# Stacked rotary query parts, one stage for the latent norms and turns, and a reordered opening in a two-block transformer kernel

## The chip, the cores and the metric

The kernel runs on one core of one Trainium2 chip. The metric is the device time of one execution in microseconds (us). TensorE (PE) multiplies matrices and accumulates in PSUM banks; VectorE (DVE) and ScalarE (ACT) read PSUM and SBUF; SyncE (SP) issues nearly all DMAs; GpSimd (POOL) does little here.

## The reference, cut to what matters

Two transformer blocks follow one another on 512 latent and 256 context rows of width 1024. The changed code lies in the first block's opening (its modulation) and in the attention of the second block's last layer, multi-head latent attention:

```python
def mla_mixer(h_ctx, h_lat, ctx_queries, w_down, q_norm, kv_norm, w_uq, w_ukv, w_o):
    rope = rope_tables(S)
    qa_l, kva_l, kr_l = mla_down(h_lat, w_down)          # 384 + 256 + 64 columns; the same for h_ctx
    k_c, v_c = mla_kv(kva_c, kr_c, kv_norm, w_ukv, None)
    k_l, v_l = mla_kv(kva_l, kr_l, kv_norm, w_ukv, rope) # rmsnorm, product, turn of the 64 rotary columns
    q_l = mla_q(qa_l, q_norm, w_uq, rope)                # rmsnorm, product; 8 heads of 128 + 64, the 64 turned
    ...                                                  # keys: context and latent, 768 in all
    s = einsum('bqhd,bkhd->bhqk', q, k) * MLA_SCALE      # contraction over 128 plain + 64 rotary columns
    o = einsum('bhqk,bkhd->bqhd', softmax(s), v)
    y_lat = o @ w_o
```

The opening computes `silu(c) @ w_ada` for the first 2048 columns and the sums of squares of the six 128-row tiles of `ctx` and `x`. All arithmetic is f32.

## The kernel before

The program is a chain of stages. A stage (`stage`, line 48) is a block in which every engine runs its own list of instructions, ordered among engines by semaphores; the next begins when all engines, SP too, have reached the end. The order is the order in which the code is written; no planner moves anything. `Chain` (line 70) makes DVE wait for its own last instruction.

**Products.** `products` (line 170) with `split` splits every f32 operand in a leading part, rounded by ACT to the type fp32r (L320), and a rest, subtracted by DVE (L335). Each product is then three matmuls: rest by leading, leading by rest, leading by leading (L398). DVE copies each finished PSUM bank (`read`); `visited` and `trailing` are hooks that run once for each visit of a result, in an engine's own order. A result whose weights come in two `k_chunks` is visited twice and read at the second.

**Opening** (`opening`, line 954). SP issues the small tables, then three of four 2 MB weight blocks of `w_ada`, then the six row tiles (0.5 MB each), the fourth block, the first weights of the next products (`bring_ahead`, line 158) and eight tables. PE multiplies each block as it lands (L1010), PE and DVE turn the results in columns (L1003, L1039), and ACT squares the six row tiles (L994).

**Latent attention** (`latent_attention`, line 3008). Products with `mla_w_down` give `qa` (4 tiles of 384) and `kva` (6 tiles of 320, the last 64 the rotary key); both lie in `m.oT`, so the trace names them `oT`. Then come stages in which almost only DVE works: `head_norms` twice, `rope` for the key (four tiles in turn) and a copy of the key to both halves of 128 columns (`kr2`). `transposes`, `halves` and the query products follow: 8 results of plain queries, 4 of rotary ones; then `rope` turns the rotary ones, `transposes` puts a pair of heads in the 128 rows of `qrT`, and the products of keys and values follow. In `attention` an item is one head and one tile of 128 queries, 32 in all. For each, PE makes scores for 768 keys in a piece of 512 and one of 256 columns (L827), turns the exponentials (L835) and multiplies by the values (L841); DVE takes the maximum (L903, L906) and scales (L910), ACT takes exponentials (L878) and copies (L895). PE's order is: turns of item i, scores of item i+2, values of item i. `HeadParts` (line 737) splits the operands of the next head on ACT and DVE between items (L764, L770). The rotary query of a head has 64 rows, 0 to 63 in even heads and 64 to 127 in odd ones; each score piece is three matmuls over 128 rows (`kn`, `qn`) and three over 64 (`kr`, `qr`).

Of the kernel before, what the change touches and what calls it, by code (L numbers as in the profile page):

```python
# [6 lines left out]
ALU = mybir.AluOpType  # L7
# [4 lines left out]
P = 128  # L12
# [132 lines left out]
def first_weights(a):  # L145
# [7 lines left out]
            (a["mla_w_down"][:, 0:384], 0, 4, 384), (a["mla_w_uq"][:, 0:512], 0, 3, 512), (a["mla_w_ukv"][:, 0:512], 0, 2, 512),  # L153
# [583 lines left out]
class HeadParts:  # L737


    def __init__(self, nc, m, ctx):  # L740
        self.nc, self.m = nc, m
        self.kn, self.qn, self.qr = [[[ctx.enter_context(nc.sbuf_tensor(f"{name}_{part}_{q}", [P, n], F32R, align_bytes=512)) for q in range(2)] for part in ("leading", "rest")]
                                     for name, n in (("kn", TOK), ("qn", LAT), ("qr", LAT))]
# [3 lines left out]
    def splits(self, h, step):  # L747
# [4 lines left out]
        pair = [(m.qrT[:, h // 2, :], self.qr[0][h // 2 % 2], self.qr[1][h // 2 % 2])] if h % 2 == 0 else []  # L752
        return [(m.qnT[:, h, :], self.qn[0][ring], self.qn[1][ring])] + pair
# [12 lines left out]
    def vector(self, dve, h, step):  # L766

        for i, (x, hi, lo) in enumerate(self.splits(h, step)):
            dve.wait_ge(self.rounded_sem, self.made(h, step) + i + 1)
            self.nc.vector.tensor_tensor(lo[:, :], x, hi[:, :].bitcast(F32), ALU.subtract).then_inc(self.parted_sem, 1)  # L770

    def scores(self, h, T):

        R, ring, pair = slice(HD * (h % 2), HD * (h % 2 + 1)), h % 2, h // 2 % 2
        kn, qn, qr, kr = [x[ring] for x in self.kn], [x[ring] for x in self.qn], [x[pair][R] for x in self.qr], [x[R] for x in self.kr]
        return [(q[a][:, T], k[b]) for q, k in ((qn, kn), (qr, kr)) for a, b in ((0, 1), (1, 0), (0, 0))]
# [177 lines left out]
def opening(nc, m, a):  # L954
# [2053 lines left out]
def latent_attention(nc, m, a):  # L3008

    with ExitStack() as ctx:  # L3010
        m.v, m.knT, m.krT, m.qnT, m.qrT = buffers(nc, ctx, v=[NT, D], knT=[8, TOK], krT=[1, TOK], qnT=[8, LAT], qrT=[4, LAT])
# [263 lines left out]
```

## Time and profile before

| | |
|---|---|
| median of 3 runs | 3911.74 us (3910.73 to 3914.24) |
| profiled execution | 3914.91 us, its span 3912.9 us |
| PE busy | 3472.2 us, 89% of the span |
| DVE busy | 1710.4 us, 44% |
| ACT busy | 970.5 us, 25% |
| mean granted TensorE clock | 0.934 |

The span is what the profiler saw from the first to the last instruction; a little time lies outside it. Shares over the span are averages of some hundred stages with different limits, so the places that the change touches have to be read by themselves: 0 to 46 us, 3120 to 3281 us and 3281 to 3452 us.

### The profile page before, as it was taken

To read this page: it belongs to the slowest core of one execution; us is meant where nothing else is said; L and a number is where in the kernel's file an instruction comes from. 1 tells how busy PE (TensorE), PEld (TensorE's weight loads), DVE (VectorE), ACT (ScalarE), POOL (GpSimd) and SP (SyncE) were. 2 spreads that over 40 slices of the span, in tenths; PEclk is the share of its full clock that TensorE was granted. 3 is DMA by queue.
4 is the path that set the end of the run, shared out by engine and by line. 5 is a ranking of instruction groups with operands and counts; after the bars stand their busy time and mean duration, and the time that the engine had idled before them with its cause. 6 is when DMAs were issued, how large, how long until landed. Compare 5 with 4: busy or idle time off the path is not lost. (4 is left out here: it accounts for less than half of the span.)

```text
span 3912.9 us, 66460 instructions
## 1 busy us (share of the span) xinstructions
PE 3472.2 (89%) x28958; PEld 2734.9 (70%) x28958; DVE 1710.4 (44%) x2847; ACT 970.5 (25%) x1647; POOL 38.7 (1%) x48
## 2 busy tenths in 40 slices
PE   5969997988998999996989977899999878989998
PEld 3858995756767655554846846788878766777877
DVE  3655554572254111114545257544443355355643
ACT  2135441242222111112011142211122212433322
POOL 0000000000000000000000000000000000000000
PEclk7979997998997999998999988999999988999999
DMA  6130003603254899993521101244432110013332
GB/s 237 60 135 4 4 4 106 191 10 111 89 189 174 356 410 408 411 410 108 178 79 60 55 2 43 68 128 119 113 106 65 46 43 28 1 44 97 97 100 89
DMA packets 254322, 486.84 MB, mean 124 GB/s; under 512 B 12394, under 2 KB 148107, under 8 KB 245364
## 3 DMA queue, kind: packets, MB, share of 16 engines
q1 hardware_dynamic: 246964, 457.91, 33.5%
q0 software_dynamic: 1984, 16.81, 1.1%
q10 hardware_dynamic: 5120, 8.39, 0.6%
q8 instruction: 201, 3.29, 0.3%
q14 instruction: 53, 0.43, 0.0%
HBM read 453.68 MB, written 29.39 MB: 123 GB/s over the span
## 5 line engine op out<-in xcount | busy, mean ns | idle before, releaser
L398 PE MATMUL banks<-leading,w_rest 128*128 128x512 f32 (+2 forms) x2016 | 735.4, 365 | 65.8 <-DVE w_rest L335 65.1
L398 PE MATMUL banks<-rest,w_leading 128*128 128x512 f32 (+2 forms) x2016 | 724.6, 359 | 0.0
L398 PE MATMUL banks<-leading,w_leading 128*128 128x512 f32 (+2 forms) x2016 | 722.5, 358 | 0.0
L335 DVE TENSOR_TENSOR w_rest<-land,w_leading 128x1024 fp32r<-128x1024 f32 (+2 forms) x344 | 321.8, 977 | 515.2 <-ACT w_leading L320 515.2
L398 PEld LDWEIGHTS banks<-leading,w_rest 128*128 128x128 f32 (+1 forms) x2016 | 384.5, 191 | 138.9 <-DVE w_rest L335 46.4
L320 ACT CAST w_leading<-land 128x1024 fp32r<-128x1024 f32 (+2 forms) x344 | 275.7, 849 | 722.2 <-DMA land<-in_w_in 242.4
L398 PEld LDWEIGHTS banks<-leading,w_leading 128*128 128x128 f32 (+1 forms) x2016 | 384.1, 191 | 57.5
L398 PEld LDWEIGHTS banks<-rest,w_leading 128*128 128x128 f32 (+1 forms) x2016 | 384.9, 191 | 54.3
L398 PE MATMUL banks<-w_rest,leading 128*128 128x512 f32 (+3 forms) x772 | 296.7, 384 | 46.1 <-DVE w_rest L335 46.1
L398 PE MATMUL banks<-w_leading,rest 128*128 128x512 f32 (+3 forms) x772 | 291.8, 378 | 0.0
L398 PE MATMUL banks<-w_leading,leading 128*128 128x512 f32 (+3 forms) x772 | 290.5, 376 | 0.0
L398 PEld LDWEIGHTS banks<-w_rest,leading 128*128 128x128 f32 x772 | 150.2, 195 | 77.7 <-DVE w_rest L335 42.4
L398 PEld LDWEIGHTS banks<-w_leading,leading 128*128 128x128 f32 x772 | 149.7, 194 | 25.1
L398 PEld LDWEIGHTS banks<-w_leading,rest 128*128 128x128 f32 x772 | 150.3, 195 | 22.9
L2345 DVE TENSOR_TENSOR y<-banks,expert_gate 128x512 f32<-128x512 f32 x32 | 35.0, 1094 | 276.4 <-PE banks L2288 276.4
L2288 PE MATMUL banks<-wd,hT 128*64 128x512 f32 x512 | 125.4, 635 | 26.9 <-ACT hT L2312 26.9
L2273 PE MATMUL banks<-wg,xT 128*64 128x256 f32 x1024 | 118.0, 384 | 1.2 <-ACT xT L2300 1.2
L2273 PE MATMUL banks<-wu,xT 128*64 128x256 f32 x1024 | 116.0, 379 | 0.0
L2273 PEld LDWEIGHTS banks<-wg,xT 128*64 128x64 f32 x1024 | 74.6, 139 | 52.3 <-issue 20.7
L398 PE MATMUL banks<-w_rest,first_up_leading 128*128 128x512 f32 x264 | 104.3, 395 | 5.7 <-DVE w_rest L335 5.7
L3106 ACT ACTIVATE first_up<-first_up 128x256 f32<-128x256 f32 (+1 forms) x44 | 23.1, 524 | 339.3 <-DVE first_up L1299 339.3
L398 PE MATMUL banks<-w_leading,first_up_rest 128*128 128x512 f32 x264 | 104.0, 394 | 0.0
(582 smaller groups left out, 5063.8 us busy)
## 6 DMA issues: line engine op xcount, KB each, us to landing
wg<-in_w_exp_gate SPq DMA_DIRECT2D x32, 2048.0 KB, 12.9
wu<-in_w_exp_up SPq DMA_DIRECT2D x32, 2048.0 KB, 14.9
wd<-in_w_exp_down SPq DMA_DIRECT2D x32, 2048.0 KB, 11.8
ws<-in_ada_w SPq DMA_DIRECT2D x96, 512.0 KB, 3.8
land<-in_w_in SPq DMA_DIRECT2D x41, 1024.0 KB, 5.4
land<-in_ffn_up SPq DMA_DIRECT2D x44, 512.0 KB, 5.3
land<-in_ffn_up SPq DMA_DIRECT2D x88, 256.0 KB, 3.3
ws<-in_w_ada SPq DMA_DIRECT2D x32, 512.0 KB, 3.8
```

Source lines behind the costliest of these rows:

```text
L320: nc.scalar.copy(leading[s % 2][:, k0:k1, 0:n], slots[s % wslots][:, k0:k1, 0:n]).then_inc(rounded_sem, 1)
L335: nc.vector.tensor_tensor(rest[s % 2][:, k0:k1, 0:n], slots[s % wslots][:, k0:k1, 0:n], leading[s % 2][:, k0:k1, 0:n].bitcast(F32), ALU.su ...
L398: mm = nc.tensor.matmul(bank_of(r, kind, at), lhsT, rhs, start=(k == 0 and q == 0), stop=(k == kt - 1 and q == len(each) - 1))
L2273: mm = nc.tensor.matmul(m.ps[SLOTS * c:SLOTS * (c + 1), bank, half(u)], b.xT[:, k, S], w[u][:, k, half(c)], start=(k == 0), stop=(k == KD ...
L2288: mm = nc.tensor.matmul(m.ps[SLOTS * n:SLOTS * (n + 1), 5 + u, :], b.hT[:, j, SLOTS * c:SLOTS * (c + 1)], wd[u][:, k, n * 512:(n + 1) * 51 ...
L2345: nc.vector.tensor_tensor(y[u][:, :].rearrange("q (f p) -> q f p", p=P), m.ps[:, 5 + u, :].rearrange("q (f p) -> q f p", p=P), e.gate[:, : ...
L3106: nc.scalar.activation(whole, whole, ACT.Silu).then_inc(aux_sem, 1)
```

## The change

Four things are done.

1. **Stacked rotary parts.** A head's rotary query is written twice, so that its transposed form `qrT` has the 64 rows twice in 128, for each of 8 heads. `HeadParts` rounds all 128 rows in place of a leading part and then overwrites rows 64 to 127 with the rest. The key is already doubled on 128 rows. So one matmul with the key's leading part gives leading by leading plus rest by leading, and another with the key's rest the other terms (the small rest-by-rest product comes along): two matmuls over 128 rows instead of three over 64. The splits of `qr` are made for each head and not for each pair, and the transposes before take 8 moves of four blocks instead of 4.
2. **One stage for norms and key turn.** The squares and sums go to ACT, as `trailing` of the down products, one tile behind DVE's copies; one square root serves both norms; the key's turn is done for four tiles at once.
3. **Query turn inside the query products.** The rotary job comes first, and DVE turns each tile at visits 4, 6, 8 and 10 of the 12; the products have 8 banks instead of 4.
4. **Opening.** The fourth weight block is issued ahead of the row tiles, and SP waits for the fifth row tile before it brings the next weights and tables.

```diff
@@ first_weights
-            (a["mla_w_down"][:, 0:384], 0, 4, 384), (a["mla_w_uq"][:, 0:512], 0, 3, 512), ...
+            (a["mla_w_down"][:, 0:384], 0, 4, 384), (a["mla_w_uq"][:, 1024:1536], 0, 3, 512), ...
@@ HeadParts
-        pair = [(m.qrT[:, h // 2, :], self.qr[0][h // 2 % 2], self.qr[1][h // 2 % 2])] if h % 2 == 0 else []
-        return [(m.qnT[:, h, :], self.qn[0][ring], self.qn[1][ring])] + pair
+        return [(m.qnT[:, h, :], self.qn[0][ring], self.qn[1][ring]), (m.qrT[:, h, :], self.qr[ring], None)]
...
+            if lo is None:
+                lo, hi, x = [y[HD:P, :] for y in (hi, hi, x)]
             self.nc.vector.tensor_tensor(lo[:, :], x, hi[:, :].bitcast(F32), ALU.subtract).then_inc(self.parted_sem, 1)
...
-        return [(q[a][:, T], k[b]) for q, k in ((qn, kn), (qr, kr)) for a, b in ((0, 1), (1, 0), (0, 0))]
+        return [(qn[0][:, T], kn[1]), (qn[1][:, T], kn[0]), (qn[0][:, T], kn[0]), (qr[:, T], self.kr[1]), (qr[:, T], self.kr[0])]
@@ opening
                 for f in range(blocks):
-                    if f == blocks - 1:
-                        for q, (dst, src) in enumerate(rows):
-                            sp.dma_start(dst, src).then_inc(landed_sem[q], 16)
                     sp.dma_start(b.w[:, f, :, :], a["w_ada"]...).then_inc(w_landed_sem[f], 16)
+                for q, (dst, src) in enumerate(rows):
+                    sp.dma_start(dst, src).then_inc(landed_sem[q], 16)
+                sp.wait_ge(landed_sem[len(rows) - 2], 16)
                 bring_ahead(m, sp)
@@ latent_attention
+            rows = [m.qa[:, t, :] for t in range(NTL)] + [m.kva[:, t, 0:256] for t in range(NT)]
+            def square(act, r, read_sem, aux_sem):
+                if r:
+                    x = rows[r - 1]
+                    act.wait_ge(read_sem, r)
+                    if r >= 2:
+                        act.wait_ge(aux_sem, r - 1)
+                    nc.scalar.activation(junk[:, 0:x.shape[1]], x, ACT.Square, accum_out=m.latent_sums[:, r - 1:r]).then_inc(aux_sem, 1)
...
-            head_norms(nc, m, [(m.qa[:, :, :], None)], 384, EPS)
-            head_norms(nc, m, [(m.kva[:, :, 0:256], None)], 256, EPS)
-            rope(nc, m, [(m.kva[:, NTC + t, 256:320].unsqueeze(1), 1, t) for t in range(NTL)])
+                    for own, width in ((slice(0, NTL), 384), (slice(NTL, NTL + NT), 256)):
+                        nc.vector.tensor_scalar(m.latent_sums[:, own], m.latent_sums[:, own], 1.0 / width, EPS, ALU.mult, ALU.add).then_inc(summed_sem, 1)
+                    for h in range(4):
+                        chain(nc.vector.tensor_tensor(spare[:, :, own], kr[:, :, other], m.rope_sin[:, :, own], ALU.mult))
+                    chain(nc.vector.tensor_tensor(kr, kr, m.rope_cos[:, :, :], ALU.mult))
+                    for c in range(2):
+                        chain(nc.vector.tensor_copy(m.kr2[:, 0:NTC, C], m.kva[:, 0:NTC, 256:320]))
+                        chain(nc.vector.tensor_tensor(m.kr2[:, NTC:NT, C], kr, spare, ALU.add))
+                    dve.wait_ge(rooted_sem, 1)
+                    chain(nc.vector.reciprocal(m.latent_rstd[:, :, 0], m.latent_root[:, :]))
+                    chain(nc.vector.tensor_tensor(m.qa[:, :, :], m.qa[:, :, :], bc(m.latent_rstd[:, 0:NTL, :], 384), ALU.mult))
+                    chain(nc.vector.tensor_tensor(m.kva[:, :, 0:256], ...))
...
+            def turn_queries(eng, v, read_sem):
+                if eng is nc.vector and v in (4, 6, 8, 10):
+                    t = (v - 4) // 2
+                    nc.vector.wait_ge(read_sem, t + 1)
...
+                    for h in range(2):
+                        turned(nc.vector.tensor_tensor(quarters(spare)[:, :, :, h, :], quarters(x)[:, :, :, 1 - h, :], ...))
+                    turned(nc.vector.tensor_tensor(x, x, m.rope_cos..., ALU.mult))
+                    for c in (1, 0):
+                        turned(nc.vector.tensor_tensor(both[:, :, c, :], x, spare, ALU.add))
...
+                products(nc, m, jobs, of_halves(pair), take, "vector", banks=8, kt=3, split=True, visited=turn_queries)
```

How the instructions stand on their engines is shown at three places. First DVE behind the down products, in the kernel before (`oT` is `qa` and `kva`, `sq` the squares, `ss` their sums):

```order
L700 TENSOR_TENSOR sq<-oT 128x1536
L701 TENSOR_REDUCE ss<-sq 128x4
L703 TENSOR_SCALAR ss<-ss 128x4
L705 RECIPROCAL rstd<-root 128x4
L709 TENSOR_TENSOR oT<-oT,rstd 128x1536
L57 UNCONDITIONAL_BRANCH
L694 UNCONDITIONAL_BRANCH
L700 TENSOR_TENSOR sq<-oT 128x1536
L701 TENSOR_REDUCE ss<-sq 128x6
```

The same place of the changed kernel, DVE again (`turning` is the spare buffer of the turn, `kr_...` the doubled key):

```order
L3050 TENSOR_SCALAR latent_sums<-latent_sums 128x4
L3050 TENSOR_SCALAR latent_sums<-latent_sums 128x6
L3055 TENSOR_TENSOR turning<-oT,rope_sin 128x4x16 x4
L3056 TENSOR_TENSOR oT<-oT,rope_cos 128x4x64
L3059 COPY kr_26213<-oT 128x2x64
L3060 TENSOR_TENSOR kr_26213<-oT,turning 128x4x64
L3059 COPY kr_26213<-oT 128x2x64
L3060 TENSOR_TENSOR kr_26213<-oT,turning 128x4x64
L3062 RECIPROCAL latent_rstd<-latent_root 128x10
L3063 TENSOR_TENSOR oT<-oT,latent_rstd 128x1536
L3064 TENSOR_TENSOR oT<-oT,latent_rstd 128x6x256
```

The squares and reductions are gone from DVE, and what were four stages is one.

Second, DVE at the end of the query products, before:

```order
L3039 COPY qnT<-banks 128x512 x2
L3039 COPY qr<-banks 128x512 x4
L57 UNCONDITIONAL_BRANCH
L722 UNCONDITIONAL_BRANCH
L731 TENSOR_TENSOR swapped<-qr,rope_sin 128x16x16 x2
L733 TENSOR_TENSOR qr<-qr,rope_cos 128x512
```

And in the middle of the same products in the changed kernel (`qr_...` is the doubled rotary query):

```order
L3094 COPY qr_26216<-banks 128x8x64 x2
L3084 TENSOR_TENSOR turning<-qr_26216,rope_sin 128x16x16 x2
L3086 TENSOR_TENSOR qr_26216<-qr_26216,rope_cos 128x8x64
L3088 TENSOR_TENSOR qr_26216<-qr_26216,turning 128x8x64 x2
L3093 COPY qnT<-banks 128x512 x2
L335 TENSOR_TENSOR w_rest<-land,w_leading 128x1024
L335 TENSOR_TENSOR w_rest<-land,w_leading 128x512
```

The turn has moved from a stage of its own between the copies, where the last weights' rest (L335) now stands behind the first turned tile.

Third, PE's scores of one item, before:

```order
L827 MATMUL banks<-kn_rest,qn_leading 128x512
L827 MATMUL banks<-kn_leading,qn_rest 128x512
L827 MATMUL banks<-kn_leading,qn_leading 128x512
L827 MATMUL banks<-kr_rest,qr_leading 128x512
L827 MATMUL banks<-kr_leading,qr_rest 128x512
L827 MATMUL banks<-kr_leading,qr_leading 128x512
L827 MATMUL banks<-kn_rest,qn_leading 128x256
```

And in the changed kernel, with the second piece:

```order
L829 MATMUL banks<-kn_rest,qn_leading 128x512
L829 MATMUL banks<-kn_leading,qn_rest 128x512
L829 MATMUL banks<-kn_leading,qn_leading 128x512
L829 MATMUL banks<-kr_rest,qr_parts 128x512
L829 MATMUL banks<-kr_leading,qr_parts 128x512
L829 MATMUL banks<-kn_rest,qn_leading 128x256
```

Each piece has two rotary matmuls instead of three, over 128 rows instead of 64.

## Rows read from the trace of the kernel before

**Rows 1.** Windows: engines' busy us with counts, then granted clock, DMA share, GB/s.

```profile
3166.06:3184.42 18.36, 0.00 (x0) 0.00 (x0) 15.20 (x28) 0.41 (x2) 0.00 (x0) 0.56 0.00 0
3225.66:3235.42 9.76, 0.00 (x0) 0.00 (x0) 8.93 (x17) 0.00 (x0) 0.00 (x0) 0.71 0.00 0
3298.00:3452.00 154.00, 150.59 (x929) 116.73 (x927) 59.21 (x140) 64.17 (x110) 0.00 (x0) 1.00 0.00 1
```

**Rows 2.** Timeline of the opening: start, length, engine, line, operation, idle before.

```profile
19.28 8.38 SPq L164 DMA_DIRECT2D land<-in_w_in  x1
23.87 2.98 PE L1010 MATMUL banks<-w,cond_wide 128*32 128x512 f32 x16 [1.18 <-DMA w<-in_w_ada]
25.14 1.06 ACT L994 ACTIVATE junk<-xc_first 128x1024 f32<-128x1024 f32 x1 [16.46 <-DMA xc_first<-in_ctx]
27.71 5.40 SPq L979 DMA_DIRECT2D rope_cos<-in_rope_cos  x1
33.15 0.47 SPq L979 DMA_DIRECT2D rope_sin<-in_rope_sin  x1
36.52 0.43 SPq L979 DMA_DIRECT2D head_mask<-in_head_mask  x1
36.99 3.64 PE L1010 MATMUL banks<-w,cond_wide 128*32 128x512 f32 x16 [8.34 <-DMA w<-in_w_ada]
45.73 1.28 ACT L604 ACT_TABLE_LOAD   x1 [13.03 <-PEq L57]
```

**Rows 3.** Timeline of DVE behind the down products.

```profile
3166.38 1.76 DVE L700 TENSOR_TENSOR sq<-oT 128x1536 f32<-128x1536 f32 x1 [0.32 <-PEq L57]
3177.16 1.76 DVE L709 TENSOR_TENSOR oT<-oT,rstd 128x1536 f32<-128x1536 f32 x1
3179.89 0.22 DVE L733 TENSOR_TENSOR oT<-oT,rope_cos 128x64 f32<-128x64 f32 x1
```

**Rows 4.** Timeline of DVE in and behind the query products.

```profile
3213.34 1.82 DVE L335 TENSOR_TENSOR w_rest<-land,w_leading 128x1024 fp32r<-128x1024 f32 x2
3224.97 0.69 DVE L3039 COPY qr<-banks 128x512 f32<-128x512 f32 x1 [1.35 <-PE banks L398]
3225.98 0.89 DVE L731 TENSOR_TENSOR swapped<-qr,rope_sin 128x256 f32<-128x256 f32 x2 [0.32 <-PEq L57]
3226.90 0.69 DVE L733 TENSOR_TENSOR qr<-qr,rope_cos 128x512 f32<-128x512 f32 x1
3237.93 0.69 DVE L499 COPY qrT<-banks 128x512 f32<-128x512 f32 x1 [0.16 <-PE banks L490]
```

**Rows 5.** Timeline of PE in one item's scores (head 7).

```profile
3435.73 0.48 PE L827 MATMUL banks<-kn_rest,qn_leading 128*128 128x512 f32 x1
3436.05 0.39 PE L827 MATMUL banks<-kn_leading,qn_rest 128*128 128x512 f32 x1
3436.28 0.40 PE L827 MATMUL banks<-kn_leading,qn_leading 128*128 128x512 f32 x1
3436.60 0.49 PE L827 MATMUL banks<-kr_rest,qr_leading 64*128 64x512 f32 x1
3436.94 0.39 PE L827 MATMUL banks<-kr_leading,qr_rest 64*128 64x512 f32 x1
3437.17 0.39 PE L827 MATMUL banks<-kr_leading,qr_leading 64*128 64x512 f32 x1
3437.50 0.39 PE L827 MATMUL banks<-kn_rest,qn_leading 128*128 128x256 f32 x1
3437.72 0.28 PE L827 MATMUL banks<-kn_leading,qn_rest 128*128 128x256 f32 x1
3437.84 0.28 PE L827 MATMUL banks<-kn_leading,qn_leading 128*128 128x256 f32 x1
3438.59 1.60 PE L841 MATMUL banks<-v,aT 128*128 128x128 f32 x12
```

**Rows 6.** Waits, 3298 to 3452: who for whom, us in total, times, longest.

```profile
PE banks L827 <- DVE qr_rest L770: 1.0, 3, 0.3
```

More of the change, by code:

```diff
@@ L741, in __init__ @@
         self.nc, self.m = nc, m
[L742 to L743 removed]
+        self.kn, self.qn = [[[ctx.enter_context(nc.sbuf_tensor(f"{name}_{part}_{q}", [P, n], F32R, align_bytes=512)) for q in range(2)] for part in ("leading", "rest")]
+                            for name, n in (("kn", TOK), ("qn", LAT))]
+        self.qr = [ctx.enter_context(nc.sbuf_tensor(f"qr_parts_{q}", [P, LAT], F32R, align_bytes=512)) for q in range(2)]
         self.kr = [ctx.enter_context(nc.sbuf_tensor(f"kr_{part}", [P, TOK], F32R, align_bytes=512)) for part in ("leading", "rest")]
@@ L3019, in latent_attention @@
             products(nc, m, jobs, hT_of(m), lambda out, j, at, chain: nc.vector.tensor_copy(
-                m.kva[:, at[0], :] if j else m.qa[:, at[0] - NTC, :], out), "vector", split=True, width=384, banks=8, k_chunks=2)
-            m.kr2, m.qaT, m.kvaT, m.qr = buffers(nc, c1, kr2=[NT, P], qaT=[3, LAT], kvaT=[2, TOK], qr=[NTL, 512])
+                m.kva[:, at[0], :] if j else m.qa[:, at[0] - NTC, :], out), "vector", split=True, width=384, banks=8, k_chunks=2, trailing=square)
             m.inputs.close()
-            head_norms(nc, m, [(m.qa[:, :, :], None)], 384, EPS)
@@ L3024, in latent_attention, with _ @@
-            head_norms(nc, m, [(m.kva[:, :, 0:256], None)], 256, EPS)
-            rope(nc, m, [(m.kva[:, NTC + t, 256:320].unsqueeze(1), 1, t) for t in range(NTL)])
-            with stage(nc, done=1) as (block, done_sem):
+            m.kr2, m.qaT, m.kvaT, m.qr2, m.turning = buffers(nc, c1, kr2=[NT, P], qaT=[3, LAT], kvaT=[2, TOK], qr2=[NTL, 2 * 512], turning=[512])
+            m.qrT = ctx.enter_context(nc.sbuf_tensor("qrT", [P, 8, LAT], F32, side="right"))
+            with stage(nc, summed=1, rooted=1, chain=1) as (block, summed_sem, rooted_sem, chain_sem):
+                @block.scalar
+                def _(act):
+                    nc.scalar.activation(junk[:, 0:1], m.ident[:, 0:1], ACT.Sqrt)
+                    act.wait_ge(summed_sem, 2)
+                    nc.scalar.activation(m.latent_root[:, :], m.latent_sums[:, :], ACT.Sqrt).then_inc(rooted_sem, 1)
@@ L3035, in latent_attention @@
             w = a["mla_w_uq"]
-            jobs = [(w[:, 0:512], 512, [("T", x, P, 0, LAT) for x in range(0, 512, P)]), (w[:, 512:1024], 512, [("T", x, P, 0, LAT) for x in range(0, 512, P)]),
-                    (w[:, 1024:1536], 512, [("N", t, 512) for t in range(NTL)])]
-            with halves(nc, m.qaT) as pair:
-                products(nc, m, jobs, of_halves(pair), lambda out, j, at, chain: nc.vector.tensor_copy(
-                    m.qr[:, at[0], :] if j == 2 else m.qnT[:, 4 * j + at[0] // P, :], out), "vector", kt=3, split=True)
@@ L3041, in latent_attention @@
-            rope(nc, m, [(m.qr[:, t, :].rearrange("p (n e) -> p n e", e=HD), 8, t) for t in range(NTL)])
-            transposes(nc, m, [([m.qr[:, t, p * P:(p + 1) * P] for p in range(4)], m.qrT[:, :, t * P:(t + 1) * P], None, None) for t in range(NTL)])
+            jobs = [(w[:, 1024:1536], 512, [("N", t, 512) for t in range(NTL)]),
+                    (w[:, 0:512], 512, [("T", x, P, 0, LAT) for x in range(0, 512, P)]), (w[:, 512:1024], 512, [("T", x, P, 0, LAT) for x in range(0, 512, P)])]
@@ L3043, in latent_attention @@
+            transposes(nc, m, [([m.qr2[:, t, (4 * g + h) * P:(4 * g + h + 1) * P] for h in range(4)], m.qrT[:, 4 * g:4 * g + 4, t * P:(t + 1) * P], None, None) for t in range(NTL) for g in range(2)])
             w = a["mla_w_ukv"]
```

29 lines of the change are left out of this document (24 added, 5 removed).

## The prediction

> **What bounds the kernel now.** I read the windows first [rows 1]. In the attention of the latent block (3298 to 3452 us) PE is busy 150.6 of 154.0 us at the full granted clock (1.00, the 2.4 GHz level), DVE 59.2 and ACT 64.2: PE's own stream is the bound there. Between the down products and the transposes (3166.06 to 3184.42) PE does nothing and DVE is busy 15.2 of 18.36 us: a bare DVE chain, paid in full. The same holds for the turn of the queries (3225.66 to 3235.42, 9.76 us). In the opening the timeline [rows 2] shows a chain of transfers: the fourth weight block lands at 36.99 us, and what PE and DVE do with it ends just before the next stage begins at 45.73. These four places are in series with everything else, so a microsecond saved in one is a microsecond of the whole, unless another engine is next in line.
>
> **Opening.** The third block has landed at 23.87, the fourth at 36.99 behind three MB of row tiles: 5 MB in 13.12 us, 2.62 us a MB [rows 2]. Ahead of the rows it lands at 23.87 + 2 x 2.62 = 29.1, and its tail (to 0.5 ahead of 45.73 before, 8.2 us) is over at 37.3. The six row tiles (1.31 us each) land from 30.4 to 37.0, the fifth at 35.7. ACT's square takes 1.06 us plus the read of its sum, inside the pitch of the tiles; ACT is through at 38.4. Now SP is late: it waits for the fifth tile (35.7) and then issues the weights and eight tables. Unblocked issues are 0.43 to 0.47 us in the rows; rope_sin to the end of head_mask is 36.95 - 33.15 = 3.8 us for seven, so nine cost 4.9 [rows 2]. SP ends at 40.6, and the next stage starts 0.5 us after, at 41.1 instead of 45.73: **4.6 us saved**. The weights and tables (3.5 MB or less, 9 us) land by about 47. The next stage, the norms of six tiles, reads none of them; only its SP waits for them, beside that work, so this costs nothing; if that stage were under 6 us long, it would cost the difference. Bounds: 7.0 if SP were free (ACT's 38.4), minus 8 if SP's issues block as before (below).
>
> **Norms and key turn.** The span of 18.36 us [rows 1] goes. In its place: ACT squares the last tile after DVE's last copy, 256 wide; a 1024-wide one takes 1.06 [rows 2], so with the read of the sum about 0.6. The other nine lie beside PE's products, where ACT waits for transfers. Stage change 0.5 (0.32 is the shortest I see, [rows 3]). Then DVE: two tiny ones 0.3; four turns of 64 elements at 0.22 + 0.04 for the chain, 1.0; three of 256 elements at 0.45 (0.89 for two, [rows 4]), 1.35, with 0.1 for chains; two copies 0.5; reciprocal 0.2; two scalings at 1.76 + 0.04, 3.6 [rows 3]. That is 7.0, and the whole 8.1: **10.2 us saved**. ACT's square root lies beside the turns. Should Square want a table of its own, a load of 1.28 us (the last row of [rows 2]) comes before the root, half hidden: bound 9.5. Above, 10.7 if the last square and the stage change cost 0.5 less.
>
> **Query turn.** A result costs PE 0.69 + 1.35 = 2.04 us [rows 4]. A turned tile costs DVE 0.93 for two halves and 3 x 0.725 for the rest, 3.1 us. I followed DVE: the last result is ready at 3224.97 [rows 4], so result 3 at 3208.65, eight steps of 2.04 before, and is copied at 3209.3; turn (3212.4), two copies (3213.8), the last weights' rest 1.82 (3215.6), turn (3218.7), two copies at 0.65 (3220.0), turn, two copies (3224.4), turn, two copies (3228.9). PE wants the rest at 3216.8 and gets its first half at 3214.7; with 8 banks it waits for no copy. So PE still ends at 3224.9 and DVE at 3228.9, against 3235.42: 6.5 us. Against this stand four more moves of transposes. A move is 0.69 + 0.16 = 0.85 [rows 4] where the clock is low, so +3.4; at the full clock DVE's 0.61 to 0.69 sets it, and eight cost 1.5 more than the four slow ones, less some lead-in. PE idles 4.4 us ahead of them instead of 10, so part may run fast; I take +3.0. **3.5 us saved**, between 3.0 and 5.5; if the rest of the weights came 2 us late to PE, 1.
>
> **Attention.** One item's scores last from 3435.73 to 3438.59, 2.86 us [rows 5]. Matmuls over 128 rows follow each other at 0.23 (512 columns) and 0.12 (256). Where PE passes from 128 rows to 64, the step is 0.32 and the one after it 0.34; back to 128, 0.33 and then 0.22 instead of 0.12. Each such passage costs 0.2 us beyond the matmuls; three lie within the scores and half of one at their end (the way to the values), 0.7 in sum. The load of the weights seems to lie bare there. Stacked, all rows are 128: five products of 0.23 and five of 0.12 and 0.1 at the entry make 1.85. Saved are 0.35 for two matmuls and 0.65 of passages, 1.0 an item, 32 for 32 items. The slow start does not double it: it ends by time and holds the same work in fewer items.
>
> What is next: with 3.9 us an item instead of 4.9, DVE and ACT have 59.2 and 64.2 us plus four more splits each (4 x 0.6) for some 122 us, so neither becomes the bound. But the next head's split of qr (0.69 on DVE) now comes before every head; before, PE waited 0.3 for it three times [rows 6]. I take 0.4 for seven heads, 1.8 more, and 1.2 for ACT's additional cast, which stands ahead of a copy that PE wants for the values, with PE there 1 us earlier. **29 us saved**; 33 if nothing waits, 27 if each head loses 0.7.
>
> Here a rule speaks against most of this term. The 64-row loads [rows 5] would, by the Trainium skill (TensorE: Matmul & The Clock Gate, section LDWEIGHTS (loading the stationary operand)), cost what 128-row ones do, since only columns count; and its Part 3 gives a matmul over few rows the time of a full one. By that alone, removing two of twelve would save their streaming time and no more, the first rival. The trace agrees with it inside a run of equal rows, but not at the passages.
>
> **Sum.** 4.6 + 10.2 + 3.5 + 29 = 47.3. The profiled execution took 3914.91 us (span 3912.9) and lies 3.2 above the median of the runs, 3911.74. Its time becomes 3867.6; the median 3864.5, which I predict. Nothing later is touched: the stages behind the attention begin from the same state, 47 us earlier.
>
> **Rivals.**
> *A. Only two matmuls go.* The extra steps come from something that stays (changes of bank or of operand), not from the 64 rows. For: four of the seven odd steps stand also at a change of piece or of engine's work. Against: 3436.28 to 3436.60 is within one bank, only the row count changes. Saved per item 0.35, 11.2 in all, less 1.5 of waits: 4.6 + 10.2 + 3.5 + 9.7 = 28, giving 3883.7.
> *B. SP's issues block in the opening.* Before, the weights took 8.38 us to issue and rope_cos 5.40 [rows 2]. From 35.7 on that makes 35.7 + 8.4 + 5.4 + 3.8 = 53.3 and a start at 53.8, 8 us late instead of 4.6 early: 3877. For: the same instructions did block. Against: then 6 MB stood in the queue, now half a MB.
> *C. Slower: the clock.* With all 128 rows working in every score product and fewer pauses, the granted clock falls to the 1.2 GHz level in the attention. An item is then 7.8 instead of 3.9 us, 125 over 32. It decides from 38% of the attention on (47 of 125); in full it gives 3989. Against it: 1.00 over 154 us with half of the score products over 128 rows, and PE 98% busy [rows 1].
> *D. The turned queries starve PE.* DVE has about 20 us of work from visit 4 on against PE's 16.3; if PE waited for all of the difference, the term's 3.5 became 0: 3868, inside my own range.
>
> **How the numbers follow.** Forecast with its own range 3856 to 3874: 0.78. A 0.11, B 0.06, C 0.02, the rest 0.03 for waits that I do not see. The range, 3855 to 3884, takes in A and B. About 0.2%, 8 us, is what a measurement can tell from no change; only C and a piece of the unseen lie outside faster: faster 0.96, same 0.02, slower 0.02.
>
> **What would show it.** The next stage's table load at 41 us, with SP's last issue ahead of it and ACT's squares done; DVE's chain behind the down products 7 us with no square in it; the last turned query 4 us behind PE's last product, then eight moves; score groups of 1.85 us without the 0.32 to 0.34 steps, and PE still over 95% busy, with the work of the 154 us window [rows 1] done in some 126. I am wrong if those steps stay at 128 rows, if SP's issue of the weights is long, or if PE waits for copies or splits by more than 5 us in all.

## The result and the profile after

| | before | after |
|---|---|---|
| median of 4 runs each | 3912.65 us (3910.73 to 3914.24) | 3860.64 us (3855.86 to 3862.22) |
| profiled execution, its span | 3914.91 us, 3912.9 us | 3855.86 us, 3854.0 us |
| PE busy | 3472.2 us, 89% | 3429.4 us, 89% |
| mean granted TensorE clock | 0.934 | 0.938 |

The time after over the time before is 0.9867, with an interval of 0.9854 to 0.9879: 52.0 us faster, where 47.3 were forecast (3864.5 us, against 3860.64 now). The profiled execution of after was its fastest, 4.8 us below its median, so the two spans differ by 58.9 us. One further run of the kernel before, on the chip of the first four experiments, was in a slow state (5723.6 us, mean granted clock 0.573) and enters no ratio. I split the two spans by the same instruction in both traces:

| stretch, by its end | before | after | gained in it |
|---|---|---|---|
| opening: next stage's table load | 45.73 | 40.57 | 5.2 |
| untouched stages: last copy of the down products | 3165.57 | 3155.72 | 4.7 |
| norms and key turn: first row of the transposes | 3185.22 | 3164.95 | 10.4 |
| query products, turn, transposes: last move of `qrT` | 3240.33 | 3214.31 | 5.75 |
| keys and values: first score matmul | 3285.69 | 3258.85 | 0.8 |
| attention: last store | 3451.41 | 3392.4 | 32.2 |

None of the four parts forecast the 4.7 us in untouched stages. They lie in several places, 3.1 of them in a run of products between 915 and 936 us. From the table load to the last copy of the down products the profiled executions of all kernels here take 3113.8 to 3122.8 us (before 3119.8, after 3115.1), so most of such a difference is scatter. One piece is not: between 2916 and 2933 us of the kernel before, where products wait for weights of `ffn_down`, after is 1.7 us faster, and so is each of the eleven kernels built from it (1.6 to 1.7 us). Why stays open. The first weight block also landed at 11.73 us in this execution and at 13.14 in that of before, so of the opening's 5.2 some 1.4 came from the landing and 3.75 from the change. The changed parts then make 3.75 + 10.4 + 5.75 + 32.2 = 52.1 us. The medians differ by 52.0; that the two agree to a tenth is luck, with untouched stages that scatter by several us.

**Opening.** The timeline of after, which answers to [rows 2] (start, length, engine, line, operation, idle time before):

```profile
11.73 3.64 PE L1012 MATMUL banks<-w,cond_wide 128*32 128x512 f32 x16 [11.73 <-DMA w<-in_w_ada]
...
27.90 3.25 PE L1012 MATMUL banks<-w,cond_wide 128*32 128x512 f32 x16 [2.51 <-DMA w<-in_w_ada]
...
34.28 0.38 SPq L164 DMA_DIRECT2D land<-in_w_in  x1
34.70 0.58 SPq L981 DMA_DIRECT2D rope_cos<-in_rope_cos  x1
...
35.53 1.06 ACT L996 ACTIVATE junk<-x_first 128x1024 f32<-128x1024 f32 x1
...
38.92 1.25 SPq L981 DMA_DIRECT2D head_mask<-in_head_mask  x1
...
40.57 1.28 ACT L604 ACT_TABLE_LOAD   x1 [3.89 <-PEq L57]
```

The fourth block is multiplied at 27.90 instead of 36.99. SP is released at 34.28, its issue of the weights takes 0.38 us instead of 8.38, and its last issue ends at 40.17, 0.4 us ahead of the next stage. ACT's last squares ended at 36.6. SP sets the end.

**Norms and key turn.** DVE's timeline behind the down products, which answers to the first of [rows 1] and to [rows 3]:

```profile
3155.72 0.49 DVE L3034 COPY oT<-banks 128x320 f32<-128x320 f32 x1 [1.27 <-PE banks L398]
3157.06 0.24 DVE L3050 TENSOR_SCALAR latent_sums<-latent_sums 128x4 f32<-128x4 f32 x2 [0.85 <-PEq L57]
...
3160.38 1.76 DVE L3063 TENSOR_TENSOR oT<-oT,latent_rstd 128x1536 f32<-128x1536 f32 x1
3162.18 1.76 DVE L3064 TENSOR_TENSOR oT<-oT,latent_rstd 128x1536 f32<-128x1536 f32 x1
3164.95 3.19 DVE L501 TENSOR_SCALAR qaT<-banks,cols 128x128 f32<-128x128 f32 x12 [1.02 <-PE banks L490]
```

No square or sum is left on DVE: its chain runs from 3157.06 to 3163.94, 6.9 us, and only the two scalings are long.

**Query turn.** DVE in the end of the query products and in the transposes, which answers to the second of [rows 1] and to [rows 4]:

```profile
3206.23 1.29 DVE L3093 COPY qnT<-banks 128x512 f32<-128x512 f32 x2
3208.50 1.46 DVE L499 COPY qrT<-banks 128x512 f32<-128x512 f32 x2 [0.99 <-PE banks L490]
3210.12 0.69 DVE L499 COPY qrT<-banks 128x512 f32<-128x512 f32 x1 [0.16 <-PE banks L490]
...
3211.83 2.48 DVE L499 COPY qrT<-banks 128x512 f32<-128x512 f32 x4 [0.16 <-PE banks L490]
```

DVE is through with its copies at 3207.52; eight moves follow (the rows are of 2, 1, 1 and 4), first 0.85 us from one to the next, then 0.60.

**Attention.** The timeline of PE in one item's scores and values, which answers to [rows 5]:

```profile
3310.79 0.49 PE L829 MATMUL banks<-kn_rest,qn_leading 128*128 128x512 f32 x1
3311.11 0.39 PE L829 MATMUL banks<-kn_leading,qn_rest 128*128 128x512 f32 x1
3311.34 0.39 PE L829 MATMUL banks<-kn_leading,qn_leading 128*128 128x512 f32 x1
3311.57 0.40 PE L829 MATMUL banks<-kr_rest,qr_parts 128*128 128x512 f32 x1
3311.80 0.40 PE L829 MATMUL banks<-kr_leading,qr_parts 128*128 128x512 f32 x1
3312.04 0.27 PE L829 MATMUL banks<-kn_rest,qn_leading 128*128 128x256 f32 x1
3312.15 0.28 PE L829 MATMUL banks<-kn_leading,qn_rest 128*128 128x256 f32 x1
...
3312.63 1.50 PE L843 MATMUL banks<-v,aT 128*128 128x128 f32 x12
```

Read the starts, one below the other. From the second on they are 0.23 apart with 512 columns and 0.11 to 0.12 with 256; the step from plain to rotary (3311.34 to 3311.57) is like all others, where it was 0.32 and then 0.34. From the first score to the values are 1.84 us instead of 2.86, and the values take 1.50 instead of 1.60.

PE's weight loads (PEld) show where the odd steps came from. Before, the two loads at a change of rows:

```profile
3436.60 0.18 PEld L827 LDWEIGHTS banks<-kr_rest,qr_leading 64*128 64x128 f32 x1 [0.36 <-issue]
3437.49 0.19 PEld L827 LDWEIGHTS banks<-kn_rest,qn_leading 128*128 128x128 f32 x1 [0.37 <-issue]
```

and after, the load for the first rotary matmul:

```profile
3311.34 0.19 PEld L829 LDWEIGHTS banks<-kr_rest,qr_parts 128*128 128x128 f32 x1
```

After, this load starts together with the matmul before its own (3311.34), 0.23 us ahead of its own (3311.57); the other loads within a run of equal rows are ahead of their matmuls too. Before, the loads at a change of rows start only with their own matmul (3436.60, and 3437.49 beside 3437.50): they are not taken ahead.

The windows (as in [rows 1]) and the waits of the same attention, 3271 to 3393 us:

```profile
3271.00:3393.00 122.00, 116.49 (x840) 105.98 (x838) 60.50 (x139) 61.19 (x107) 0.00 (x0) 1.00 0.00 1
```

```profile
...
PEld banks L829 <- ACT e L880: 4.3, 7, 0.9
PEld banks L843 <- ACT aT L897: 4.2, 11, 1.2
PE banks L829 <- DVE qr_parts L772: 2.8, 7, 0.7
```

PE is busy 116.49 of 122 us, 95.5%, against 97.8% before. It waits seven times, once for each next head, for the rest of its rotary query, as in the row below. The 4.3 us for `e` stand at the same places; of the 4.2 us for `aT`, 2.3 belong to the last two items, as in before, and the other nine waits last 0.15 to 0.24 us. The row:

```profile
3371.39 0.47 PE L829 MATMUL banks<-kn_rest,qn_leading 128*128 128x512 f32 x1 [0.35 <-DVE qr_parts L772]
```

Best seen in the distance from one item's first score matmul to the next: before 4.88 us, with 5.46 at three heads; after, for the four items of a head, 3.74, 3.74, 3.96, 4.65. The last two hold 0.2 and 0.9 us of waits.

### The profile page after: what moved, and what is told of

Read it like the earlier page. It is cut to its first block and busy times, and to the rows that moved or that the text cites. A ratio compares the mean times of both kernels' runs of the same rounds, so it can differ in the third digit from the quotient of the medians.

```text
span 3854.0 us, 66346 instructions
## 1 busy us (share of the span) xinstructions
PE 3429.4 (89%) x28910; PEld 2721.4 (71%) x28910; DVE 1710.8 (44%) x2845; ACT 976.4 (25%) x1671; POOL 38.9 (1%) x48
## 5 line engine op out<-in xcount | busy, mean ns | idle before, releaser
L335 DVE TENSOR_TENSOR w_rest<-land,w_leading 128x1024 fp32r<-128x1024 f32 (+2 forms) x344 | 321.7, 977 | 518.1 <-ACT w_leading L320 518.1
L2290 PEld LDWEIGHTS banks<-wd,hT 128*64 128x64 f32 x512 | 35.9, 143 | 95.9 <-issue 61.4
## 6 DMA issues: line engine op xcount, KB each, us to landing
wg<-in_w_exp_gate SPq DMA_DIRECT2D x32, 2048.0 KB, 12.7
```

The lines of the kernel that those rows point to most:

```text
L335: nc.vector.tensor_tensor(rest[s % 2][:, k0:k1, 0:n], slots[s % wslots][:, k0:k1, 0:n], leading[s % 2][:, k0:k1, 0:n].bitcast(F32), ALU.su ...
L2290: mm = nc.tensor.matmul(m.ps[SLOTS * n:SLOTS * (n + 1), 5 + u, :], b.hT[:, j, SLOTS * c:SLOTS * (c + 1)], wd[u][:, k, n * 512:(n + 1) * 51 ...
```

## The experiments

All are built from the kernel after. Each time is a median, with the range and number of its runs; each ratio is to the kernel before on the same chip. The first four below shared a chip, the next four, and the last three; the kernel before had medians of 3910.49, 3914.31 and 3909.75 us there. So two medians of different chips, that of after (beside 3912.65) among them, compare to 3 or 4 us only, and a smaller difference is read from the traces.

### Three rotary matmuls over 64 rows

```diff
...
-        return [(qn[0][:, T], kn[1]), (qn[1][:, T], kn[0]), (qn[0][:, T], kn[0]), (qr[:, T], self.kr[1]), (qr[:, T], self.kr[0])]
+        R = slice(HD * (h % 2), HD * (h % 2 + 1))   # qr and kr: rows R of a leading part and of a rest
...
+        return [(q[a][:, T], k[b]) for q, k in ((qn, kn), (qr, kr)) for a, b in ((0, 1), (1, 0), (0, 0))]
```

> The changed kernel with the old form of the rotary scores: three matmuls over 64 rows a piece, split for each head. Theory (each passage of PE between 128 and 64 rows costs about 0.2 us beyond the matmuls): a score group is back at 2.86 us, the attention loses 29 to 33 us, and the time is 3890 to 3894. Rival (only the number of matmuls counts, 0.35 us an item): the loss is 11, 3872.

Measured: 3898.26 us (3893.82 to 3899.48, 7 runs), ratio 0.9968 (0.9957 to 0.9980), 37.6 us slower than after and 4 us over the expected 3890 to 3894. The odd steps are back, here on PE's timeline:

```profile
3311.52 0.40 PE L830 MATMUL banks<-kn_leading,qn_leading 128*128 128x512 f32 x1
3311.84 0.50 PE L830 MATMUL banks<-kr_rest,qr_leading 64*128 64x512 f32 x1
3312.18 0.39 PE L830 MATMUL banks<-kr_leading,qr_rest 64*128 64x512 f32 x1
...
3312.74 0.39 PE L830 MATMUL banks<-kn_rest,qn_leading 128*128 128x256 f32 x1
3312.96 0.28 PE L830 MATMUL banks<-kn_leading,qn_rest 128*128 128x256 f32 x1
```

An item takes 4.88 us as before. The attention takes 172.2 us, 6.5 more than before with the same matmuls: 2.4 are the splits for each head (0.59 at seven heads, where before had them at three), and 4.1, the miss of the expectation, lie in its first four items. The windows tell why; of this kernel:

```profile
3276.70:3282.70 6.00, 6.00 (x20) 4.15 (x19) 1.50 (x3) 2.14 (x5) 0.00 (x0) 0.50 0.01 3
3282.70:3288.70 6.00, 6.00 (x27) 4.68 (x27) 1.21 (x4) 2.46 (x5) 0.00 (x0) 0.72 0.00 0
```

of before:

```profile
3291.70:3297.70 6.00, 6.00 (x19) 4.11 (x18) 1.43 (x5) 1.66 (x3) 0.00 (x0) 0.50 0.00 0
3297.70:3303.70 6.00, 6.00 (x35) 4.42 (x34) 2.40 (x5) 3.81 (x8) 0.00 (x0) 0.98 0.02 4
```

and of after:

```profile
3258.80:3262.00 3.20, 3.15 (x9) 2.69 (x10) 0.00 (x0) 0.00 (x0) 0.00 (x0) 0.50 0.00 0
3262.00:3266.00 4.00, 3.82 (x21) 3.22 (x21) 2.29 (x5) 1.27 (x3) 0.00 (x0) 0.87 0.00 0
```

The attention began at the granted clock 0.50 (1.2 GHz) in all three, for 12 us before, 4 in after (a quarter of its second window) and 21 here (0.50 without a break from 3264.70, and 56% of the last window). The other traces fall in line: 11 us in the grouped kernel below, which has 64-row matmuls too, and 4.1 to 5.8 us in the nine others, whose score matmuls all have 128 rows.

### Three rotary matmuls over 128 rows

As above with `R = slice(0, P)`, and the second half of the key's columns zero, so that the product is the same with all 128 rows:

```diff
+                        if c:
+                            chain(nc.vector.memset(m.kr2[:, :, C], 0.0))
+                            continue
...
```

> Three rotary matmuls a piece, but all over 128 rows; the second half of the key's rows is zero, so the scores are those of the reference. Theory of the passages: a group lasts 1.85 + 0.35 = 2.2 us without steps of 0.32, so it loses 11 to 13 us against the changed kernel (3873) and is some 18 faster than the form with 64 rows. Rival (only the number of matmuls counts): no difference to the form with 64 rows.

Measured: 3869.82 us (3867.79 to 3870.86, 4 runs), ratio 0.9896 (0.9880 to 0.9913), 9.2 us slower than after, where 11 to 13 were expected: the two matmuls cost 10.9 us, and the waits at each head are 0.8 us instead of 1.1. Against the first experiment it gains 28.4 us and not 18, some 6 of them in the shorter start at the low clock. The same places on its timeline:

```profile
3338.88 0.39 PE L830 MATMUL banks<-kn_leading,qn_leading 128*128 128x512 f32 x1
3339.11 0.39 PE L830 MATMUL banks<-kr_rest,qr_leading 128*128 128x512 f32 x1
3339.34 0.39 PE L830 MATMUL banks<-kr_leading,qr_rest 128*128 128x512 f32 x1
```

As many matmuls as before, of the same columns and banks and from the same buffers, and no odd step: an item takes 4.08 us. So of the 1.14 us between 4.88 and 3.74, 0.80 come from the change of rows and 0.34 from the two matmuls. Rival A is refuted. Nor does it matter which half of the rows is used: before, items take 4.88 us in even heads (rows 0 to 63) and in odd ones (64 to 127).

### Rotary matmuls over 64 rows, grouped

The six plain matmuls of an item first, both pieces, then the six rotary ones: one change of rows within the scores and one at their end, instead of three and one.

```diff
+                        for group in (range(0, 3), range(3, 6)):
+                            for _, c, w in pieces:
+                                for j in group:
+                                    lhsT, rhs = parts[j]
+                                    mm = nc.tensor.matmul(row(i, 0)[:, c:c + w], lhsT, rhs[:, c:c + w], start=(j == 0), stop=(j == len(parts) - 1))
```

> Three rotary matmuls over 64 rows, but the plain ones of both pieces first and then the rotary ones of both: two passages an item instead of four. Theory of the passages: 0.4 us less an item than in the form with 64 rows, 13 us in all, 3878. Rival (matmuls over 64 rows are slow by themselves, wherever they stand): no difference to that form, 3891.

Measured: 3881.87 us (3879.59 to 3883.18, 4 runs), ratio 0.9927 (0.9911 to 0.9944), 16.4 us faster than the first experiment, where 13 were expected. In the traces the attention is 17.2 us shorter (154.9 instead of 172.2); 4.5 of them are the shorter start at the low clock (11 us instead of 21), so 12.7 are of the grouping. Its timeline, of every kind one row:

```profile
3336.75 0.28 PE L827 MATMUL banks<-kn_leading,qn_leading 128*128 128x256 f32 x1
3336.97 0.50 PE L827 MATMUL banks<-kr_rest,qr_leading 64*128 64x512 f32 x1
3337.30 0.39 PE L827 MATMUL banks<-kr_leading,qr_rest 64*128 64x512 f32 x1
...
3337.77 0.28 PE L827 MATMUL banks<-kr_rest,qr_leading 64*128 64x256 f32 x1
```

The first step is 0.22 instead of 0.12, the second 0.33 instead of 0.23. From 3337.30 on, two matmuls of 512 columns fill 0.47 us: 64-row matmuls are not slow among themselves. The scores take 2.47 us, 0.39 less than 2.86, for two passages less: 0.2 us for each passage, half in the step to the first matmul of the new rows and half in the next. The odd steps follow the row count and neither the bank nor the piece.

### The splits of the next head spread over three items

`kn`, `qn` and `qr` are split one to an item, `kn` and `qn` one item earlier than in after:

```diff
...
+        return [(h, step) for h in range(1, 8) for step in range(3) if max(NTL * (h - 1) - 1 + step, 0) == i]
...
-                    if heads is not None and i % NTL < 2 and i + NTL < n:
-                        heads.vector(dve, i // NTL + 1, i % NTL)
...
```

> The changed kernel with the next head's splits one to an item (kn, qn, qr) instead of two and one, beginning an item earlier. Theory (PE waits for the rest of qr at seven heads, 2.8 us in the trace, and for ACT's copy behind two casts): 3 to 5 us less in the attention, 3857. Rival (these waits are covered by others, or the casts only move them): within 1 us.

Measured: 3857.11 us (3850.76 to 3861.59, 4 runs), ratio 0.9860 (0.9844 to 0.9877). The items of a head take 3.73, 3.95, 3.75 and 4.05: the wait for the rest is gone. Of the wait below (3280 to 3398 us) 2.3 us are those of the last two items, as in before; four of 0.15 us are left within the stream, where ACT's cast for the next head still stands ahead of the copy of the turned exponentials. That this order also makes the rest of the 0.2 and 0.3 us an item is not shown here:

```profile
PEld banks L849 <- ACT aT L904: 2.9, 6, 1.2
```

The attention takes 129.8 us instead of 133.5. The medians differ by 3.5, within their ranges; that the 3.7 us come from the waits is told by the traces.

### The opening's order as before

```diff
+                    if f == blocks - 1:
+                        for q, (dst, src) in enumerate(rows):
+                            sp.dma_start(dst, src).then_inc(landed_sem[q], 16)
```

> The changed kernel with the order of transfers of the opening as it was. Theory (the next stage begins when the last engine is through, 5.2 us earlier with the change, and nothing gives it back): the next stage starts at 45.7 us and the time is 5 us over the changed kernel's, 3866. Rival (the later stages, which wait for transfers, give part of it back, as the trace suggests with 5.2 us at 41 us and 2.8 at 200): 3 us over or less.

Measured: 3863.46 us (3862.48 to 3863.56, 4 runs), ratio 0.9874 (0.9857 to 0.9890), 2.8 us slower than after. Its next stage began at 45.51 us, 32.6 after its first block had landed at 12.88, as before (32.6); in after it began 28.8 after. So the order is worth 3.8 us by these two traces. In all nine kernels that have the new opening whole, the next stage begins 28.7 to 30.9 us after the landing, 29.4 in the middle one, which makes 3.2 us. The expected 5 had counted 1.4 us of an earlier landing. The medians differ by 2.8 us, as the rival has it; between chips they can't tell that from 3.2 or from 5.

### The opening without SP's wait

```diff
-                sp.wait_ge(landed_sem[len(rows) - 2], 16)
```

> The changed opening without SP's wait for the fifth row tile; the issues follow at once. Theory (SP ended the opening at 40.2 us because it waited till 34.3; its issues would go on while the rows land, and before it was through at 36.95 with as much queued): the next stage starts at 37.5 to 38.5, with ACT's squares last, 2 to 3 us earlier. Rival (the issue of the weights and rope_cos blocks for 8.4 and 5.4 us until the queue has drained): no gain, or later than 40.6.

Measured: 3860.78 us (3858.27 to 3864.41, 4 runs), ratio 0.9868 (0.9852 to 0.9885). Its timeline:

```profile
25.02 0.64 SPq L164 DMA_DIRECT2D land<-in_w_in  x1
25.70 9.01 SPq L980 DMA_DIRECT2D rope_cos<-in_rope_cos  x1
...
39.45 1.06 ACT L995 ACTIVATE junk<-x_first 128x1024 f32<-128x1024 f32 x1
...
40.86 1.28 ACT L604 ACT_TABLE_LOAD   x1 [0.27 <-PEq L57]
```

One issue blocks for 9.01 us behind the six tiles, but it started at 25.70 and is over in time; now ACT's last squares are what ends last. The next stage began 26.7 us after the landing of the first block (14.18 here), 2.1 less than in after, as the theory has it. The median of after is 3860.64: nothing of it shows in the time, as the rival has it.

### The query turn in a stage of its own

```diff
-                products(nc, m, jobs, of_halves(pair), take, "vector", banks=8, kt=3, split=True, visited=turn_queries)
+                products(nc, m, jobs, of_halves(pair), take, "vector", banks=8, kt=3, split=True)
+            with stage(nc, unused=1) as (block, unused_sem):   # DVE: the four tiles' turns, one behind the other
...
```

> The changed kernel with the turn of the queries in a stage of its own behind the query products. Theory (beside PE's products all but 4 us of the turn are hidden): 12.4 us of turn follow the last copy instead of 4, so 8.5 to 9.5 us more, 3870. Rival (the turn between the copies delays PE's weights): less than 6 us more.

Measured: 3871.49 us (3869.56 to 3878.39, 4 runs), ratio 0.9901 (0.9884 to 0.9917), 10.9 us slower than after. From the first copy of the query products to the end of the transposes are 43.2 us instead of 32.5, so 10.6 locally. The moves begin at the low clock (granted 0.50), as they do in after:

```profile
3221.80 0.69 DVE L499 COPY qrT<-banks 128x512 f32<-128x512 f32 x1 [1.66 <-PE banks L490]
```

It is slower than the old code at this place, since the turn now writes two halves (12.3 us from its first instruction to its last instead of 9.4) and eight moves follow and not four.

### The splits begun two items earlier than in after

```diff
-        return [(h, step) for h in range(1, 8) for step in range(3) if max(NTL * (h - 1) - 1 + step, 0) == i]
+        return [(h, step) for h in range(1, 8) for step in range(3) if max(NTL * (h - 1) - 2 + step, 0) == i]
```

The diff is against the experiment with the spread splits, and all three are one item earlier than there (against after, `kn` and `qn` are two items earlier and `qr` one). ACT's cast stands behind its copy of the item and not ahead of it.

> Like the version with the splits spread over items, but begun two items earlier and with ACT's cast behind its copy. Theory (what is left of PE's waits there, 0.3 us for the rest of qr and 0.2 for the copy behind a cast at each head, goes): all items last 3.74 us, 3.5 us less in the attention, 3854. Rival (a later cast makes the next exponential late): items of 3.74 us grow, no gain.

Measured: 3851.82 us (3850.37 to 3853.26, 4 runs), ratio 0.9843 (0.9827 to 0.9860), 8.8 us faster than after. From the fourth on, every item takes 3.74 to 3.75 us. The windows show a PE without a gap:

```profile
3300.00:3380.00 80.00, 80.00 (x601) 75.43 (x600) 43.27 (x99) 43.29 (x77) 0.00 (x0) 1.00 0.01 1
```

The attention takes 125.3 us, 8.2 less than in after. These 8.2 us are what the head's preparation cost there. How much of the last 4.5 us, against the spread splits, is of the earlier item and how much of ACT's order is not told apart.

### The norms, key turn and copies as before

```diff
-                ... "vector", split=True, width=384, banks=8, k_chunks=2, trailing=square)
+                ... "vector", split=True, width=384, banks=8, k_chunks=2)
...
+            head_norms(nc, m, [(m.qa[:, :, :], None)], 384, EPS)
+            head_norms(nc, m, [(m.kva[:, :, 0:256], None)], 256, EPS)
+            rope(nc, m, [(m.kva[:, NTC + t, 256:320].unsqueeze(1), 1, t) for t in range(NTL)])
...
```

> The changed kernel with the norms, the key's turn and its copies as they were, in four stages of DVE alone. Theory (a bare DVE chain, paid in full): 18.4 us between the last down copy's end and the end of the key's copies instead of some 8, so 10.3 us more, 3871. Rival (the squares that ACT takes beside the down products delay its weights there, and so give part back): less than 9 us more.

Measured: 3872.74 us (3866.50 to 3873.97, 4 runs), ratio 0.9907 (0.9892 to 0.9922), 12.1 us slower than after by the medians and 10.6 by the profiled spans (3864.6 and 3854.0). Two rows of DVE, the last copy of the down products and the first of the transposes:

```profile
3156.00 0.49 DVE L3034 COPY oT<-banks 128x320 f32<-128x320 f32 x1 [1.27 <-PE banks L398]
...
3175.66 3.19 DVE L501 TENSOR_SCALAR qaT<-banks,cols 128x128 f32<-128x128 f32 x12 [0.81 <-PE banks L490]
```

They are 19.66 us apart (before 19.65, after 9.23), so the part is worth 10.4 us.

### Four banks in the query products

```diff
-... of_halves(pair), take, "vector", banks=8, kt=3, split=True, visited=turn_queries)
+... of_halves(pair), take, "vector", banks=4, kt=3, split=True, visited=turn_queries)
```

> The changed kernel with 4 banks instead of 8 in the query products. Theory (DVE turns a tile for 3.1 us between copies and reads results up to 4 us late, so PE would have to wait for a bank): with 4 banks a result may be at most 8 us late, which it isn't by more than a fraction, so 0 to 1 us more. Rival (the eight banks carry the hidden turn): 3 us more or above.

Measured: 3861.51 us (3859.53 to 3862.15, 4 runs), ratio 0.9875 (0.9860 to 0.9891), against 0.9867 (0.9854 to 0.9879) for after: no difference that can be told. In the traces the stretch from the first row of the transposes to the last move of `qrT` is the same, 49.3 us beside 49.4: PE did not need the additional banks.

### Early splits and no wait in the opening

The eighth and the sixth experiment together.

> The changed kernel with the splits begun two items earlier behind ACT's copy, and without SP's wait in the opening. Both gains measured alone (8.2 us in the attention, 2.2 in the opening when counted from the landing of the first weight block) should add up: 3850. Rival (the opening's gain is lost to transfers of later stages): 3852, as with the splits alone.

Measured: 3847.84 us (3846.80 to 3851.14, 5 runs), ratio 0.9843 (0.9830 to 0.9857). It is the fastest of all and beats both kernels: after by 12.8 us of medians, or by 9.4 from the ratios (0.0024 of 3912). The items take 3.74 to 3.75 us again. Beside the early splits alone the median is 4.0 us lower, but the ratio is the same, 0.9843, the kernel before being faster on this chip too. The next stage after the opening began at 38.37 us, 25.3 after the landing at 13.08 and 3.5 less than in after; whether this is still worth anything at the end stays open, since neither ratios nor medians show it.

## Why the prediction was right

The time, the order of the terms and their mechanisms came out; the forecast was 4.7 us short, from sizes that lean to both sides. The closeness is luck in part: 1.7 us of the gain lie in a place that no term names, and three misses in the attention cancel in part.

**Opening, 4.6 forecast, 3.75 measured.** The fourth block was forecast at 29.1 and the fifth row tile at 35.7 from a landing of the first block at 13.14. With the landing at 11.73 they came at 27.90 and 34.28, that is 29.3 and 35.7 when shifted by 1.4. What was mis-sized is SP: its nine issues took 5.9 us and not 4.9, with one of 1.25. In the middle one of the nine kernels with this opening the gain is 3.2. Rival B did not come about (0.38 us for the weights). The kernel without the wait shows the same queue blocking for 9.01 us, so the rival priced something real, and it is the half MB left in flight that made the issue free here.

**Norms and key turn, 10.2 forecast, 10.4 measured.** DVE's chain was forecast at 7.0 and took 6.9. No table load came before the square root.

**Query turn, 3.5 forecast, 5.75 measured.** DVE was to end 4 us behind PE's last product and ended 3.2 behind (the first copy at 3181.77 plus the 22.54 us between first and last result of before gives 3204.3, against 3207.52). The four additional moves were to cost 3.0 and cost 1.9: from DVE's last row to the end of the moves are 6.8 us, 4.9 before. The moves passed to the pace of the full clock half way (0.85 us from one to the next, then 0.60). That was said to be possible and taken at too little; that PE's shorter idle time did it is argued only. The remaining 0.4 lie ahead of the first copy. Rival D did not come about: from the first copy to the end of PE's last product are 22.4 us, as before (22.5).

**Attention, 29 forecast, 32.2 measured.** Three sizes were off, one of them the other way. Rival C did not come about: the granted clock is 1.00 from 3271 to 3393 us.

1. An item's scores fell to 1.84 us as forecast (1.85), but the item gained 1.14 and not 1.0, 4.5 us more over 32. The forecast counted three and a half passages. The half that was left out, behind the entry of the values, is the 0.10 us by which these are now shorter.
2. The waits for the next head grew by 6.5 us (8.2, less the 1.7 of before) and not by 3. Each head costs 0.9 us in one item and 0.2 in the item before. The rows name 0.4 us a head for DVE's split, exactly as taken (2.8 in all), but where PE waits for it, the turns and the first score lie 1.18 us apart instead of 0.57: the item loses 0.6, as it did before (5.46 instead of 4.88), and the wait row shows only part of it (with the splits spread, 0.3 of the 0.6 are still there). That is 4.2 - 1.7 = 2.5 us more, and not 1.8. The term that failed is the 1.2 us for ACT: the values, which wait for ACT's copy behind its casts, begin up to 0.2 us later and last 0.1 longer in two items of each head, and what lies there makes the other 4 us. "PE waits for copies or splits by more than 5 us in all" was named as a sign of being wrong; it happened, and the attention's gain came out above its forecast all the same, by points 1 and 3.
3. "The slow start does not double it: it ends by time" failed. The start at 1.2 GHz lasted 4 us instead of 12 and gave back 2.5 us: the first three items took 16.6 us before and 10.6 in the kernel with early splits, 6.0 less, of which 3 x 1.14 are the matmuls. Its length goes with the rows of the score matmuls: 11, 12 and 21 us in the three kernels with 64-row matmuls, 4.1 to 5.8 in the ten with 128 rows throughout. So these 2.5 us belong to the stacking as well, as far as one trace of each kernel tells; by what means stays open.

Together 36.5 - 6.5 + 2.5 = 32.5, beside 32.2 measured.

**The rows.** The central claim, that a passage between 128 and 64 rows costs 0.2 us beyond the matmuls, is shown by three kernels: with 64 rows the steps are there, with 128 rows and all else equal they are not, and with half as many passages half of them is. That the load of the weights lies bare there, as I wrote, agrees with the rows of PEld: at a passage the load starts with its own matmul and not with the one before. Why PE doesn't take it ahead stays open. The rule weighed in the prediction, of the Trainium skill (TensorE: Matmul & The Clock Gate, section LDWEIGHTS (loading the stationary operand)), that only the columns count in a load, agrees with the trace within a run of equal rows (what I took from its Part 3 stands on that page under "Why this matters for your kernels"): loads of 64 and of 128 rows last 0.18 and 0.19 us, and 64-row matmuls of 512 columns follow each other at 0.23 like those of 128. By it alone the stacked kernel would have stood at 3883.7.

**Undoing one part** gives 2.8, 12.1, 10.9 and 37.6 us by medians. They sum to 63 and not to 52, since the last two leave in place what the change added for them (eight moves and a turn that writes twice; splits for each head), and the last also ran through a longer start at the low clock.

## What to carry to other kernels

Within a stream of matmuls keep the number of contracted rows the same: stack two parts in 128 rows, and where that can't be, put the matmuls of equal rows together. When a stream gets shorter, the work that other engines do for its next piece must begin earlier as well; here that cost more (8.2 us) than moving the query turn gained (5.75). For a change of one per cent, read each part between two instructions next to it in both traces, since untouched stages differed by up to 9 us between the kernels' profiled executions.

## What the runs showed of the hardware that was not expected

- At a change between 128 and 64 contracted rows, the step to the first matmul of the new rows and the step after it each grow by 0.1 us, in both directions, and the load of the weights at the change starts with its own matmul instead of one matmul ahead.
- The granted clock of 0.50 at the start of the attention lasted 11, 12 and 21 us in the three kernels whose scores have 64-row matmuls and 4.1 to 5.8 us in the ten with 128 rows throughout, though all do nearly the same before it. Between 12 and 21 us lie 4.1 us of time.
- SP's issue of one and the same small table took 0.58 us when it waited for the fifth row tile first and 9.01 when it didn't.
